# Gate 1 spread ahead of the pooled product, unit 5 of the modulation around the router, first expert rows turned ahead of its spreads

## The reference, cut to what matters

```python
m = jax.nn.silu(cvec) @ w_mod + b_mod            # six vectors: shift1, scale1, gate1, shift2, scale2, gate2
h = x * (1 + scale1) + shift1
y = pool_mixer(h)                                 # layer 0; a gated DeltaNet in layer 1
x = layer_norm(alpha * x + gate1 * y)
h = x * (1 + scale2) + shift2
scores = sigmoid(h @ w_router)                    # top 2 of 16 experts inside one group of 4
x = layer_norm(alpha * x + gate2 * moe(h))
```

## Time and profile before

| | us |
|---|---|
| median of three runs | 927.09 (926.78 to 927.1) |
| the profiled execution | 931.07 |
| its span, first to last instruction | 929.2 |
| TensorE busy | 761.4 (82%) |
| VectorE busy | 427.7 (46%) |
| ScalarE busy | 336.2 (36%) |
| GpSimd busy | 291.1 (31%) |
| TensorE's granted clock, mean | 0.905 of full |

### The profile page before, as it was taken

The page is one execution under the profiler, slowest core; times in us unless marked ns, Lnnn a source line. Parts: engine busy times, 40 slices in busy tenths (PEclk is TensorE's granted clock), DMA queues, the critical chain, the costliest instruction groups (busy, mean ns, idle before and its releaser), DMA issues. The chain is left out here.

```text
span 929.2 us, 14984 instructions
## 1 busy us (share of the span) xinstructions
PE 761.4 (82%) x5209; PEld 456.5 (49%) x5209; DVE 427.7 (46%) x1039; ACT 336.2 (36%) x776; POOL 291.1 (31%) x702
## 2 busy tenths in 40 slices
PE   0978859999999258899999999999898538999970
PEld 0544425555555104545666665765656224555530
DVE  0039553121121494642677677777744742121116
ACT  0231322222222215544557565575641122222221
POOL 0000112333333200084345746548440021333330
PEclk9989959999999669995899999999997757999995
DMA  9999999999694499384441423513110399999913
GB/s 242 407 374 391 402 396 368 375 365 345 250 377 160 170 401 302 111 303 153 103 129 43 126 75 91 143 42 112 42 57 1 132 410 347 361 391 382 371 66 120
DMA packets 100578, 219.29 MB, mean 236 GB/s; under 512 B 28311, under 2 KB 63455, under 8 KB 89505
## 3 DMA queue, kind: packets, MB, share of 16 engines
q1 hardware_dynamic: 91551, 200.39, 61.3%
q0 software_dynamic: 8224, 15.75, 5.1%
q10 hardware_dynamic: 740, 2.32, 0.9%
HBM read 212.09 MB, written 17.33 MB: 247 GB/s over the span
## 5 line engine op out<-in xcount | busy, mean ns | idle before, releaser
L1203 PE MATMUL banks<-h_cols,weight_ring 128*128 128x512 f32 (+1 forms) x384 | 161.0, 540 | 0.7
L1180 POOL TENSOR_TENSOR arena<-arena 128x60 f32<-128x60 f32 (+24 forms) x248 | 80.9, 326 | 126.1 <-DMA arena<-blocks 107.3
L808 DVE TENSOR_TENSOR arena<-arena,banks 128x128 f32<-128x128 f32 x42 | 12.0, 287 | 203.4 <-ACT arena L779 203.4
L866 POOL DMA_INDIRECT y_of_tokens<-arena,place_now x42 | 44.3, 1054 | 169.3 <-ACT arena L786 169.3
L1182 POOL TENSOR_TENSOR arena<-arena 128x60 f32<-128x60 f32 (+24 forms) x248 | 84.8, 342 | 19.4
L1203 PEld LDWEIGHTS banks<-h_cols,weight_ring 128*128 128x128 f32 x384 | 66.6, 195 | 34.7 <-issue 31.7
L286 PE MATMUL banks<-weight_ring,c_cols 128*32 128x512 f32 x368 | 52.1, 680 | 31.4 <-DMA weight_ring<-in_w_mod_dram 31.3
L844 POOL DMA_INDIRECT arena<-h_of_tokens,row_now x50 | 49.3, 985 | 86.3 <-DVE place_of_slot L713 38.6
L774 ACT COPY arena<-arena 64x1024 f32<-64x1024 f32 x46 | 48.1, 1046 | 77.2 <-PE banks L732 58.2
L751 PE MATMUL banks<-weight_ring,arena 128*64 128x256 f32 x576 | 67.9, 390 | 1.1 <-ACT arena L774 1.1
L732 PE MATMUL banks<-const,arena 64*128 64x64 f32 x352 | 57.1, 285 | 13.0 <-ACT arena L774 13.0
(11 more groups left out here) (293 smaller groups left out, 1342.4 us busy)
## 6 DMA issues: line engine op xcount, KB each, us to landing
weight_ring<-in_w_mod_dram SPq DMA_DIRECT2D x46, 1024.0 KB, 9.8
weight_ring<-in_dn_w_in_dram SPq DMA_DIRECT2D x32, 512.0 KB, 7.0
weight_ring<-in_w_gate_dram SPq DMA_DIRECT2D x13, 1024.0 KB, 11.2
weight_ring<-in_w_up_dram SPq DMA_DIRECT2D x13, 1024.0 KB, 14.3
weight_ring<-in_w_down_dram SPq DMA_DIRECT2D x13, 1024.0 KB, 17.6
arena<-in_w_gate_dram SPq DMA_DIRECT2D x7, 1024.0 KB, 12.5
arena<-in_w_up_dram SPq DMA_DIRECT2D x7, 1024.0 KB, 14.7
arena<-in_w_down_dram SPq DMA_DIRECT2D x7, 1024.0 KB, 17.0
```

Source lines behind the costliest of these rows:

```text
L866: pool.indirect_dma_start(y_halves, bass.IndirectOffsetOnAxis(m.place_now[:, u:u + 1], 0), v.y_tile[u], None, bounds_check=last_row, oob_i ...
L1180: then(pool.tensor_tensor(part, U[:, 0:q, j:j + 1].to_broadcast([P, q, BLK - 1 - j]), M[:, j, j + 1:BLK].unsqueeze(1).to_broadcast([P, q, ...
L1203: mm = pe.matmul(bank(6 + j % 2)[:, 0:CTX + SEQ - n0], head_w[h % 2][:, j, k, :], m.hT[:, k, n0:CTX + SEQ], start=(k == 0), stop=(k == KD ...
```

## The change

Four edits of order, and one added instruction.

1. VectorE sums unit 1 (gate 1) after the sixth of eight scaled columns, and TensorE spreads it ahead of the first pooled product instead of after it.
2. ScalarE makes a sigmoid of a small unused operand at the start of `act_router`, in both layers.
3. Of unit 5's eight steps, two instead of five stand in the router's first gap, three instead of three others in the second, and the last three behind the router's last product.
4. TensorE turns the first expert's rows ahead of unit 5's four spreads, and ScalarE copies the first rows ahead of the copies of those spreads. ScalarE's warm-up silu in `act_moe` thereby also comes ahead of them.

```diff
-        def pe_router(pe, L, beside=lambda: None, behind=lambda: None):
+        def pe_router(pe, L, beside=lambda: None, behind=lambda: None, last=lambda: None):
...
             mm.then_inc(s("router_mm"), 1)
+            last()
 
         def act_router(act, L):
             t_ = L.tag
+            act.activation(m.c_silu[:, :], m.c_rows[:, :], ACT.Sigmoid)
...
-        def pe_moe(pe, L):
+        def pe_moe(pe, L, first_turned=lambda: None):
...
             turn(0, KD).then_inc(s("turned_first"), 1)
+            first_turned()
             pe.wait_ge(s("router_meta"), L.n + 1)
...
-        def act_moe(act, L):
+        def act_moe(act, L, first_copied=lambda: None):
...
             act.wait_ge(s(t_ + "rows0"), 16)
             copied(0)
+            first_copied()
             act.wait_ge(s("turned_first"), L.n + 1)
...
             act_mod(act, 4)
-            act_mod(act, 5)
-            act_moe(act, L0)
+            act_moe(act, L0, lambda: act_mod(act, 5))
...
+            pe_mod_spread(pe, 1, 0)
             pe_pool_y(pe, 0)
-            pe_mod_spread(pe, 1, 0)
             pe_pool_y(pe, 1)
...
             def in_router():
                 pe_mod_spread(pe, 4, 0)
-                beside([(5, i) for i in range(5)])
-            pe_router(pe, L0, in_router, lambda: beside([(5, i) for i in range(5, KD)]))
-            pe_mod_spread(pe, 5, 0)
-            pe.wait_ge(s("mod_ready"), READY_END[5])
-            pe_moe(pe, L0)
+                beside([(5, i) for i in range(2)])
+            pe_router(pe, L0, in_router, lambda: beside([(5, i) for i in range(2, 5)]), lambda: beside([(5, i) for i in range(5, KD)]))
+
+            def first_turned():
+                pe_mod_spread(pe, 5, 0)
+                pe.wait_ge(s("mod_ready"), READY_END[5])
+            pe_moe(pe, L0, first_turned)
...
             for c in range(KD):
                 dve_scale(dve, c)
-            dve_mod(dve, 1)
+                if c == KD - 3:
+                    dve_mod(dve, 1)
             dve.wait_ge(s("mod_ready"), READY_END[1])
```

## The result

The changed kernel takes 930.63 us (median of 9 runs, 929.08 to 932.7) against 927.09 (9 runs, 925.48 to 928.99) for the kernel before on the same chip: a ratio of 1.0039, 95% interval 1.0027 to 1.0052. It is slower, by 3.5 us, where 926.8 was forecast and 929.2 was the top of the range. The profiled execution has a span of 929.1 us and took 930.96, close to the median.

What follows compares the result with a forecast made beforehand. TensorE's work bounds the first layer's expert loop, so only its first tile's start counts: 0.3 us later there, -0.62 in the second layer, -0.3 in all. From 931.07 to 930.8, less 3.98: 926.8 us; range 924.4 to 929.2.

Steps and rivals of the forecast that it cites:

- The 5.4 us that the router gains: First layer's router: places' product starts at 118.85 against 124.27, so the gather is issued and lands 5.4 us sooner.
- the spreads that lost their cover: Entry to first layer's expert loop: four spreads with copies, formerly under the gather's flight, now cost 5.93 us at half clock.
- Pooling: Pooling stage: unit 1's earlier sum and spread make TensorE's stream 0.5 to 0.95 us earlier; 0.7 taken.
- rival (c): Both routers: a table switch costs about 2.66 us, more than its row; 924.0, or 924.2 by a pause; chance 0.03.
- The 0.18 and 0.62 taken from the rows: Routers: moving the sigmoid's table load ahead of the copies saves 0.18 us in the first layer, 0.62 in the second.
- Unit 5: First layer's router: counting product 2.9 us sooner, second gap's three steps hidden, places' product 5.4 us sooner, last three steps behind it.
- 3.98 us: Whole kernel: profiled execution's 931.07 us less the three runs' median of 927.09; subtracted from the summed 930.8 to give 926.8.
- if it takes its 7.6 us again: First layer's gather: issued at 122.5, it lands at 130.1 if its flight takes 7.6 us as before.
- rival (b): Half clock lasts longer: first tile costs 1.1 to 2.0 us more; with the pooled product caught too, 929.3; chance 0.19.
- Rival (a): Half clock ends sooner, by the first tile's start (1.6 less) or in pooling (2.0 less): -2.8, 924.3; chance 0.22.
- (d): Change hidden: spreads run under something, or unit 5's later place gives nothing; worth -5.9 or +5.4 us; chance 0.03.

Runs made afterwards that it cites:

- run b: The kernel before, unchanged, profiled again (one of three further profiles); its own time was 926.39 us.

## Why the prediction was wrong

The step that failed is the balance at the end of the change's parts: "The 5.4 us that the router gains pay for the spreads that lost their cover." Both sides of it were mis-sized, the gain the more. By the timed runs the first three edits together gave 2.6 and 4.8 us (ratios 0.9972 and 0.9948) where the sum has 6.2 (0.7 + 4.7 + 0.2 + 0.6 in the table below), and the turn edit cost 6.9 where it has 5.9. Per term, with the mean of the four profiles of before as the base:

| term | forecast | measured |
|---|---|---|
| pooling, to the first transpose | -0.7 | -1.9 (97.9 to 96.0) |
| first transpose to gather | -4.7 | -2.4 (27.3 to 24.9) |
| flight of the gather | -0.2 | +0.6 (8.25 to 8.85) |
| copy of rows to first tile | +5.9 | +6.7 (3.44 to 10.14) |
| length of the first tile | 0 | +0.9 (5.53 to 6.40; without the turn edit 6.41 and 6.39) |
| layer 1 | -0.6 | 0 (all behind the first tile's end: 784.6 to 784.7) |
| sum | -0.3 | +3.9; own times 926.98 to 930.96, +4.0; medians +3.5 |

The measured column sets one execution against four, so single rows can be off by a microsecond; that it adds up to the medians' difference within 0.4 us is in part luck.

**Pooling: right mechanism, small gain larger than taken.** VectorE's gate came at 63.5 as forecast and the tiles still waited for TensorE. The size goes with the instant at which the clock returned: set against the execution of before in which it returned as early (63.7), the first transpose is 0.5 us sooner, and not 1.9. All seven profiles with unit 1's spread in its old place have the first transpose at 96.5 to 98.8 (mean 97.8), the seven with it moved at 95.3 to 98.0 (mean 96.5): about 1.4 us.

**Sigmoid: right that rival (c)'s pause is not there.** The Trainium skill (ScalarE: Activation LUTs, What ACT_TABLE_LOAD costs) would have had the two layers give 1.6 and 2.0 us, as the prediction estimates; the trace does not agree. The edit alone measured 1.0004, and its interval ends at 1.5 us gained. In the changed kernel's trace a load at 107.85 (1.28 us) is followed by its activation at 109.14; no drain shows. The 0.18 and 0.62 taken from the rows are too small to be told from nothing by the times. In layer 1 the clock took most of the second in the changed kernel, and with the sigmoid alone it came as far as the gather's issue but not to the tile (above).

**Unit 5: right about the weights and the count, wrong about the second gap and about the kernel before.** The gather was forecast 24.4 us after the first transpose and came at 24.9; the six profiles with the edit and without the held loads lie between 24.85 and 24.96. That it came so near is in part luck. Up to the counting product the forecast is exact (12.8 us). From there to the places' product it has 8.0 and 9.3 were measured: three steps were to fill the second gap "hidden" in 2.7 us, but from 111.3 to 118.1 TensorE had half clock, they took 5.35, and the places' product waited 0.8 for them. Then that product ran at full clock, which gave 0.8 back on the 1.93 us taken for it. In the kernel before, run b, the half clock lies from 117.3 to 120.7, and the operands are ready 7.9 us after the counting product and not 8.5: so against run b the gather comes 1.8 us sooner (26.7 to 24.9 behind the first transpose), less than the 2.2 us that the count gained.

But the 29.1 from which 24.4 was subtracted is not what the kernel before usually takes: 26.5 to 26.8 in three of four profiles, 26.0, 27.8 and 29.5 in three kernels that share this code. The 5.4 us contained some 2.4 us of half clock and late weights of one execution. The same text then subtracted 3.98 us to come from that execution to the median, and so used the execution's ill luck twice: once as a gain that the change would bring, once as an excess that the median would not have.

**The gather "if it takes its 7.6 us again".** It did not: 8.9 us to the copy. (The sum's 0.03 us from landing to copy stands in no row; the earlier trace rows have 0.23, from 135.48 to 135.71, which matters little.) How much of the stretch the expert loads in front of it cause stays open (above).

**The turn ahead of the spreads: the lost cover was priced rightly, one cost was missed.** The block took 5.92 us for 5.93. Behind it TensorE's register loads, hidden before under ScalarE's work, followed its new last wait: 2.05 us from the last copy to the tile, of which the copy of rows that follows explains some 1.0.

**The first tile: the first half of rival (b).** The half clock went on through the tile, to 145.4, and it took 6.40 us. It is not the turn edit's doing alone: the tile takes 6.39 to 6.41 us without that edit, 6.17 with unit 5's edit alone, 6.10 with the turn alone, and 5.18 in the changed kernel with the counts read ahead; in the kernel before and with the first or the second edit alone it takes 5.21 to 5.74. Which edit lengthens it stays open. The second half of (b), a pooled product caught at half clock all through, did not occur, and its 929.3 rested on the same base. (Rival (a)'s -2.8 from 926.8 would be 924.0; its 924.3 counts from the kernel before.)

Rival (a)'s clock came in the pooling, not in the tile. (c) is refuted by the sigmoid's ratio. Of (d), that the spreads run under something after all is refuted by the 10.14 us from copy to tile; that unit 5's later place gives nothing is not excluded by its own ratio, and the traces give it half of what was counted.

Left open: why the half clock of the pooling and the router lies at other places in executions of the same code, and what made the excess between the two expert stages in the profile used.

## What to carry to other kernels

A gain read off waits in one profile is only as typical as that profile. If its own time is well above the median, look for the excess in the very stretches that the change removes, and do not both count them as gain and subtract the offset; a second profile of the unchanged kernel would have shown here that the router gave 2.4 us, not 4.7, against 6 to 7 for the cover taken away. Work called hidden at full clock may not be hidden at half. And when a wait is moved to just before the critical instruction, everything behind it on that engine comes onto the path, register loads too. Reading them just ahead of the spreads gave back 0.4 us; a place where TensorE waits anyway, ahead of its wait for the gathered rows, was not tried.

## What the runs showed of the hardware

- With the reading of two counts into TensorE's registers between its last wait and the tile, the tile started 2.05 us after the last copy of the spreads (2.04 with nothing else to wait for); with the reading ahead of the spreads it started 1.00 us after it, 0.06 us after the copy of rows, and TensorE stood idle for 0.59 us at the new place.
- The same code got its half clock in other places: in the pooling 60.4 to 67.2, 60.2 to 63.7, 62.7 to 66.1 and 61.9 to 65.3 in four executions of the kernel before. In the changed kernel three of unit 5's steps took 5.35 us in the router at half clock, in the kernel before five took 4.50 at full clock. 29 runs of it on one chip differed by 7.65 us (922.06 to 929.71).
- A gather of 64 rows was copied 7.8 to 8.6 us after its issue in the kernel before, which issues it at 123.3 to 127.9, 8.6 to 9.1 in six kernels that issue it at 120.2 to 122.3, and 7.9 in the one kernel that held the second expert's loads until 0.9 us before it.
